# Hybrid attention in double items of both token tiles

## The reference

```python
def one_block(q_blk):                         # differential attention, 128 queries
    s = jnp.einsum('bqhcd,bkhcd->bhcqk', q_blk, k).astype(jnp.float32) * scale
    p = jax.nn.softmax(s, axis=-1)
    a = p[:, :, 0] - lam * p[:, :, 1]
    return jnp.einsum('bhqk,bkhe->bqhe', a.astype(v.dtype), v)
...
of = of * lax.rsqrt(jnp.mean(jnp.square(of), axis=-1, keepdims=True) + RMS_EPS)
...
m = jnp.maximum(jnp.max(s, axis=-1, keepdims=True), sk)      # windowed attention
e = jnp.exp(s - m)
p = e / (jnp.sum(e, axis=-1, keepdims=True) + jnp.exp(sk - m))
o = jnp.einsum('bnhgqk,bnkhd->bnqhgd', p.astype(v.dtype), vb)
```

## Time and profile before

| | |
|---|---|
| median of three runs | 1758.63 us (1757.71 to 1762.2) |
| profiled execution: span, and all that is known of its time | 1762.7 us |
| TensorE busy | 1706.5 us (97%) |
| VectorE, ScalarE, GpSimd busy | 921.5, 631.6, 107.9 us |
| attention of layer 0 | from about 250 to 294 us |
| attention of layer 1 | from about 744 to 790 us |

### The profile page before, as it was taken

How to read it: one execution, slowest core, us unless ns; L and a number is a source line. 1 busy time by engine, 2 the same in 40 slices (tenths; PEclk the granted TensorE clock), 3 DMA queues, 4 the chain that set the end, 5 groups by cost and what they waited for, 6 DMA issues and landing times.

```text
span 1762.7 us, 21725 instructions
## 1 busy us (share of the span) xinstructions
PE 1706.5 (97%) x8752; PEld 1235.5 (70%) x8752; DVE 921.5 (52%) x1313; ACT 631.6 (36%) x824; POOL 107.9 (6%) x89
## 2 busy tenths in 40 slices
PE   8999999999999999999999998999998999999996
PEld 7888877878878888878887787744443777644442
DVE  4754757675465546676685597511113667411113
ACT  4544444364434443443554364211112344211110
POOL 1000060000000000512000000000000000000000
PEclk9999999999999999989999999999999999999998
DMA  7555540645555545505554343999999443999995
GB/s 304 188 191 189 193 168 1 239 180 182 188 202 187 184 189 189 193 25 202 187 183 167 137 176 120 363 413 426 428 428 380 173 144 115 363 413 424 430 424 240
DMA packets 47667, 419.77 MB, mean 238 GB/s; under 512 B 5377, under 2 KB 5377, under 8 KB 9185
## 3 DMA queue, kind: packets, MB, share of 16 engines
q1 hardware_dynamic: 44064, 405.82, 59.0%
q0 software_dynamic: 3520, 12.78, 2.1%
HBM read 417.53 MB, written 1.05 MB: 237 GB/s over the span
## 4 chain that ended last, share of the span: by engine, by line
PE 81%; DVE 7%; DMA 6%; ACT 3%; POOL 1%; issue 1%; SPq 0%; DVEq 0%; POOLq 0%; ACTq 0%
PE hh L1282 10%; PE y L659 10%; PE y L660 10%; PE y L661 10%; PE hh L659 8%; PE hh L661 8%; PE hh L660 8%; DMA wide<-pairs 6%; PE turn L1192 2%; PE hh L1314 2%; PE turn L1314 2%; DVE w_lo L1921 2%; ACT w_hi L1469 1%; PE y L1326 1%; PE turn L779 1%; PE turn L691 1%
## 5 line engine op out<-in xcount | busy, mean ns | idle before, releaser
L1921 DVE TENSOR_TENSOR w_lo<-raw,w_hi 128x2048 fp32r<-128x2048 f32 x181 | 411.2, 2289 | 141.5 <-ACT w_hi L1469 140.8
L1469 ACT ACTIVATE w_hi<-raw 128x2048 fp32r<-128x2048 f32 x193 | 365.0, 1912 | 58.1 <-DMA raw<-units 58.0
L659 PE MATMUL hh<-w_hi,xt_hi 128*128 128x512 f32 x704 | 279.6, 397 | 4.4 <-ACT work L1721 2.1
L661 PE MATMUL hh<-w_hi,xt_lo 128*128 128x512 f32 x704 | 275.3, 391 | 0.0
L660 PE MATMUL hh<-w_lo,xt_hi 128*128 128x512 f32 x704 | 274.8, 390 | 0.0
L1282 PE MATMUL hh<-wide,work 128*64 128x512 f32 x880 | 196.0, 594 | 4.1 <-DMA wide<-pairs 4.1
L659 PE MATMUL y<-w_hi,xt_hi 128*128 128x512 f32 (+1 forms) x464 | 183.4, 395 | 4.8 <-DVE xt_lo L2470 3.1
L660 PE MATMUL y<-w_lo,xt_hi 128*128 128x512 f32 (+1 forms) x464 | 179.4, 387 | 0.0
L661 PE MATMUL y<-w_hi,xt_lo 128*128 128x512 f32 (+1 forms) x464 | 179.2, 386 | 0.0
L659 PEld LDWEIGHTS hh<-w_hi,xt_hi 128*128 128x128 f32 x704 | 132.7, 188 | 33.6 <-DVE xt_lo L2028 2.9
L661 PEld LDWEIGHTS hh<-w_hi,xt_lo 128*128 128x128 f32 x704 | 132.4, 188 | 28.3
(11 more groups left out here) (366 smaller groups left out, 1994.8 us busy)
## 6 DMA issues: line engine op xcount, KB each, us to landing
raw<-units SPq DMA_DIRECT2D x193, 1024.0 KB
wide<-pairs SPq DMA_DIRECT2D x81, 2048.0 KB
wide<-pairs SPq DMA_DIRECT2D x8, 1024.0 KB, 9.9
late<-pairs SPq DMA_DIRECT2D x7, 1024.0 KB
raw<-pairs SPq DMA_DIRECT2D x7, 1024.0 KB
spare<-pairs SPq DMA_DIRECT2D x2, 2048.0 KB
xt_wide<-pairs SPq DMA_DIRECT2D x2, 2048.0 KB
ln_gb<-ln_g POOLq DMA_DIRECT2D x6, 512.0 KB, 3.9
```

The source lines that it names most:

```text
L659: pe.matmul(dst, left[0], right[0], start=start, stop=False)
L661: return pe.matmul(dst, left[1], right[0], start=False, stop=stop)
L1469: act.activation(hi[r][:, :], raw[r][:, :], ACT.Copy).then_inc(hi_ready, 1)
L1921: dve.tensor_tensor(lo[r][:, :], raw[r][:, :], hi[r][:, :].bitcast(F32), ALU.subtract)\
```

## The change

TensorE, VectorE and ScalarE now work on double items j of both token tiles. `scores(j)` writes four score matrices, tile 0 into the first and tile 1 into the second half of each bank; `score[j % 2]` is reused by double item j + 2. `maxima(j)` is one reduction of 1024 columns into four maxima, and `combine(j)` computes the two ratios at once and then issues two weighted differences. The exponential buffers are four instead of two. The copies of the turned items are shared: the even ones (tile 0) go to ScalarE, the odd ones (tile 1) to VectorE, in the differential and in the windowed part. The squares for the norm move to GpSimd (`mix_squared`). The loop of TensorE goes `turn(i)`, `pv(i - 1)`, and after each odd i `scores(i // 2 + 2)`; `scores(0)` and `scores(1)`, now of four items, still stand in the middle of the last tile of the projection.

The diff, cut to its core (unchanged lines, new semaphores and the renumbered waits of `pv` are left out, and some indentation):

```diff
@@ -431,7 +432,7 @@
-e1 = carve(work, 11520, 2, 2, T)
+e1 = [carve(work, at, 2, T) for at in (11520, 12032, 13056, 13568)]
...
@@ -602,6 +603,9 @@
+        for t in range(TT):
+            pool.wait_ge(diff_read, TT * l + t + 1)
+            pool.tensor_tensor(rot[:, t], mix[:, t, 0:512], mix[:, t, 0:512], ALU.mult).then_inc(mix_squared, 1)
...
@@ -885,24 +889,27 @@
     def hybrid(l):
-        def scores(i):
-            t = i % 2
-            k_tile = i // 2 if i < 8 else 4 + (i - 8) // 4
-            if i >= 2:
-                pe.wait_ge(exp_ready, 16 * l + i - 1)
-            if i == 1:
+        def scores(j):
+            if j >= 2:
+                pe.wait_ge(exp_ready, 16 * l + 2 * j - 2)
+            if j == 1:
                 pe.wait_ge(tile_taken, seen(tile_taken, TT))
-            if i == 8:
+            if j == 4:
                 pe.wait_ge(col_ready, seen(col_ready, 2))
-            for c in range(2):
-                rows = slice(HD * c, HD * c + HD)
-                mm = pe.matmul(score[t][:, c, 0:T], qt1[rows, i // 2, t * P:(t + 1) * P], kt1[rows, k_tile, :],
-                               start=True, stop=i < 8)
-            if i >= 8:
-                other = slice((1 - t) * P, (2 - t) * P)
+            k_tile = j if j < 4 else 4 + (j - 4) // 2
+            for t in range(TT):
+                for c in range(2):
+                    rows = slice(HD * c, HD * c + HD)
+                    mm = pe.matmul(score[j % 2][:, c, t * T:(t + 1) * T], qt1[rows, j, t * P:(t + 1) * P],
+                                   kt1[rows, k_tile, :], start=t == 0, stop=t == 1 and j < 4)
+            if j >= 4:
                 pe.wait_ge(masks_ready, 6)
-                for c in range(2):
-                    mm = pe.matmul(score[t][:, c, other], ident_r[:, :], swa_far[:, t, other], start=False, stop=True)
+                for t in range(TT):
+                    other = slice((1 - t) * P, (2 - t) * P)
+                    for c in range(2):
+                        mm = pe.matmul(score[j % 2][:, c, t * T + (1 - t) * P:t * T + (2 - t) * P], ident_r[:, :],
+                                       swa_far[:, t, other], start=False, stop=t == 1)
             mm.then_inc(scores_ready, 1)
...
@@ -923,10 +930,7 @@
-            if i < 8:
-                pe.wait_ge(pt_ready, seen(pt_ready))
-            else:
-                pe.wait_ge(swa_pt, 8 * l + i - 7)
+            pe.wait_ge((pt_ready, odd_pt)[t], 8 * l + i // 2 + 1)
...
@@ -1595,30 +1599,35 @@
         def exps(i):
-            b = i % 2
-            act.wait_ge(neg_ready, seen(neg_ready))
-            if 2 <= i < 10:
-                act.wait_ge(prob_ready, 8 * l + i - 1)
-            elif i >= 10:
-                act.wait_ge(prob_turned, 16 * l + i - 1)
+            t, j = i % 2, i // 2
+            if t == 0:
+                act.wait_ge(neg_ready, seen(neg_ready))
+            if 4 <= i < 12:
+                act.wait_ge(prob_ready, 8 * l + i - 3)
+            elif i >= 12:
+                act.wait_ge(prob_turned, 16 * l + i - 3)
             for c in range(2):
-                head = i // 2 if i < 8 else 2 * ((i - 8) // 2) + c
-                neg, total = (neg_diff[:, b, c], diff_sum[:, b, c]) if i < 8 else (neg_swa[:, b], swa_sum[:, b])
-                ins = act.activation(e1[:, b, c], score[b][:, c, 0:T], ACT.Exp, bias=neg[:, head:head + 1],
-                                     accum_out=total[:, head:head + 1])
+                head = j if i < 8 else 2 * (j - 4) + c
+                neg, total = (neg_diff[:, t, c], diff_sum[:, t, c]) if i < 8 else (neg_swa[:, t], swa_sum[:, t])
+                ins = act.activation(e1[i % 4][:, c], score[j % 2][:, c, t * T:(t + 1) * T], ACT.Exp,
+                                     bias=neg[:, head:head + 1], accum_out=total[:, head:head + 1])
             ins.then_inc(exp_ready, 1)
...
             act.wait_ge(prob_turned, 16 * l + i + 1)
-            act.activation(pt1[:, i % 2, 0:T], turn_bank[i % 2][:, 0:T], ACT.Copy).then_inc(pt_ready, 1)
-        for i in range(16):
-            exps(i)
-            if i == 15:
-                act.wait_ge(sink_ready, l + 1)
-                act.activation(sink_e, sink_e, ACT.Exp).then_inc(sink_exp, 1)
-            if 2 <= i < 10:
-                copies(i - 2)
+            n_ = T if i < 8 else 2 * T
+            act.activation(pt1[:, 0, 0:n_], turn_bank[0][:, 0:n_], ACT.Copy).then_inc(pt_ready, 1)
+        for j in range(8):
+            exps(2 * j)
+            if j >= 2:
+                copies(2 * j - 2)
+            exps(2 * j + 1)
+            if j == 1:
+                copies(0)
+        copies(14)
+        act.wait_ge(sink_ready, l + 1)
+        act.activation(sink_e, sink_e, ACT.Exp).then_inc(sink_exp, 1)
         for b in range(2):
...
@@ -2117,28 +2126,31 @@
-        def maxima(i):
-            b = i % 2
+        def maxima(j):
             dve.wait_ge(scores_ready, seen(scores_ready))
-            s = score[b][:, :, 0:T]
-            if i < 8:
-                dve.tensor_reduce(neg_diff[:, b, :, i // 2], s, AX_X, ALU.max, negate=True).then_inc(neg_ready, 1)
+            s = score[j % 2][:, :, :].rearrange("p c (t k) -> p t c k", t=TT)
+            if j < 4:
+                dve.tensor_reduce(neg_diff[:, :, :, j], s, AX_X, ALU.max, negate=True).then_inc(neg_ready, 1)
             else:
-                two = slice(2 * ((i - 8) // 2), 2 * ((i - 8) // 2) + 2)
-                link(dve.tensor_reduce(nmax[:, b], s, AX_X, ALU.max, negate=True))
-                dve.tensor_tensor(neg_swa[:, b, two], nmax[:, b], neg_sink[:, l, two], ALU.min)                            .then_inc(neg_ready, 1)
-        def combine(i):
-            b, h = i % 2, slice(i // 2, i // 2 + 1)
-            dve.wait_ge(exp_ready, 16 * l + i + 1)
-            link(dve.reciprocal(ratio[:, b], diff_sum[:, b, 1, h]))
-            link(dve.tensor_scalar(ratio[:, b], ratio[:, b], diff_sum[:, b, 0, h], minus_lam[:, l:l + 1],
-                                   ALU.mult, ALU.mult))
-            if i >= 2:
-                dve.wait_ge(prob_turned, 16 * l + i - 1)
-            dve.scalar_tensor_tensor(out=p1[:, b], in0=e1[:, b, 1], scalar=ratio[:, b], in1=e1[:, b, 0],
-                                     op0=ALU.mult, op1=ALU.add).then_inc(prob_ready, 1)
+                two = slice(2 * (j - 4), 2 * (j - 4) + 2)
+                sinks = neg_sink[:, l, two].rearrange("p (o h) -> p o h", o=1).broadcast_to([P, TT, 2])
+                link(dve.tensor_reduce(nmax, s, AX_X, ALU.max, negate=True))
+                dve.tensor_tensor(neg_swa[:, :, two], nmax, sinks, ALU.min).then_inc(neg_ready, 1)
+        def combine(j):
+            dve.wait_ge(exp_ready, 16 * l + 2 * j + 2)
+            if j > 0:
+                dve.wait_ge(prob_ready, 8 * l + 2 * j)
+            link(dve.reciprocal(ratio, diff_sum[:, :, 1, j]))
+            link(dve.scalar_tensor_tensor(out=ratio, in0=ratio, scalar=minus_lam[:, l:l + 1], in1=diff_sum[:, :, 0, j],
+                                          op0=ALU.mult, op1=ALU.mult))
+            for t in range(TT):
+                i = 2 * j + t
+                if i >= 2:
+                    dve.wait_ge(prob_turned, 16 * l + i - 1)
+                dve.scalar_tensor_tensor(out=p1[:, t], in0=e1[i % 4][:, 1], scalar=ratio[:, t:t + 1], in1=e1[i % 4][:, 0],
+                                         op0=ALU.mult, op1=ALU.add).then_inc(prob_ready, 1)
...
@@ -2153,10 +2165,9 @@
-        def square(t):
-            dve.wait_ge(diff_read, TT * l + t + 1)
-            link(dve.tensor_tensor(rot[:, t], mix[:, t, 0:512], mix[:, t, 0:512], ALU.mult))
+        def sum_squares(t):
+            dve.wait_ge(mix_squared, TT * l + t + 1)
             dve.tensor_reduce(ssq[:, t], heads(rot[:, t]), AX_X, ALU.add).then_inc(squares, 1)
...
@@ -2170,26 +2181,24 @@
             dve.wait_ge(prob_turned, 16 * l + i + 1)
-            dve.tensor_copy(pt1[:, i % 2, :], turn_bank[i % 2][:, :]).then_inc(swa_pt, 1)
-        for i in range(16):
-            if i == 2:
+            n_ = T if i < 8 else 2 * T
+            dve.tensor_copy(pt1[:, 1, 0:n_], turn_bank[1][:, 0:n_]).then_inc(odd_pt, 1)
+        for j in range(8):
+            maxima(j)
+            if j >= 2:
+                copies(2 * j - 3)
+            if 1 <= j < 5:
+                combine(j - 1)
+            if j == 1:
                 values()
-            maxima(i)
-            if i >= 10:
-                copies(i - 2)
-            if 1 <= i < 9:
-                combine(i - 1)
-            if i in (9, 10):
-                read_diff(i - 9)
-            if i in (11, 12):
-                square(i - 11)
-            if i in (13, 14):
-                sub_norm(i - 13)
-        dve.wait_ge(neg_ready, seen(neg_ready, 16))
+            for t in range(TT):
+                if j >= 5:
+                    (read_diff, sum_squares, sub_norm)[j - 5](t)
+        dve.wait_ge(neg_ready, seen(neg_ready, 8))
```

(19 more changed lines are left out.)

## The result

| kernel | median us | runs | ratio to before (95% interval) | mean clock of the profiled run |
|---|---|---|---|---|
| before | 1761.98 | 5 | 1 | 0.988 |
| changed | 1803.48 | 5 (1794.98 to 1805.66) | 1.0236 (1.0219 to 1.0254) | 0.973 |

The change makes the kernel 41.5 us slower. Slower was forecast, but by 24.4 us; 1803.5 lies just above the range's upper end of 1801. The forecast of 1783 stood on 1758.6 for the kernel before, the median of three runs; with two more runs that median is 1762.0, so 3.4 us of the miss are the base and 17.1 the change. The profiled run took 1803.48 us with a span of 1801.4.

The account below looks back on a forecast made before the run. It took a dependency ring over two items, not any engine's work, to bound the differential part. Base 1758.6 plus 20.4 for the new order and 4 for low clock gave 1783 us; range 1776 to 1793, 8 in 10 1768 to 1801.

Parts of the forecast that it names:

- The ring through combine, turn, product, scores and maxima: Differential part: each double's combination must return as scores before the next, 5.6 us per double against 3.47.
- The windowed part, 6.0 per double at full clock: Windowed attention: odd product waits for VectorE's copy behind the maxima; 6.0 us per double, 1.4 more.
- The start: Start of attention: GpSimd's low part holds combine(0)'s second difference until 260.27, values end at 262.3, double 2's scores at 265.0.
- The squares on GpSimd: Norm squares on GpSimd: 1.15 us each, two end at 288 before the sums at 290.7, so they cost nothing.
- The sum, 20.4: Both layers' attention without further low-clock stretches: last product of layer 0 at 302.4 instead of 292.20, 10.2 us per layer.
- The clock, 4 us: TensorE in both attention stages: two low-clock stretches per layer beyond the start's, about 1 us each.
- the clock stays low: Rival, chance 0.15: new gaps keep TensorE at 1.2 GHz for most of both stages, 13 us per layer, 1805 us.
- The profiled span: Whole kernel before: span 1762.7 us, three-run median 4.1 below, about what layer 1's slow end costs.

Follow-up runs that it names:

- e8_fill_both: Changed kernel plus 12 unread matmuls at each of five TensorE waits per layer, in the differential and windowed parts: 1783.79 us, 1.0143 of before.
- e5_low_parts_moved: `e1_scores_ahead` with the low parts of units 7 and 8 per attention layer on VectorE instead of GpSimd: 1744.15 us, 0.9903 of before.
- e1_scores_ahead: Changed kernel with scores(j + 2) issued ahead of turn(2j) instead of behind turn(2j + 1) on TensorE: 1748.15 us, 0.9922 of before.
- e6_squares_back: `e1_scores_ahead` with the two squares of the norm back on VectorE instead of GpSimd: 1756.04 us, 0.9977 of before.
- e2_fill: Changed kernel plus 12 unread matmuls ahead of turn(2), turn(4) and turn(6) per layer, where TensorE waits: 1790.19 us, 1.0164 of before.
- e7_copies_unshared: `e1_scores_ahead` with copies as before the change, ScalarE all differential and VectorE all windowed items: 1766.97 us, 1.0022 of before.

## Why the prediction was right in kind and wrong in size

- *The ring through combine, turn, product, scores and maxima.* Right. The waits stand where it said, the order undone removes them, and its 5.6 us, 6.3 for the double with masks, were measured as 5.4, 5.8 and 6.0 once the clock was kept. (Its terms add up to 5.7.)
- *The windowed part, 6.0 per double at full clock.* Right: in `e8_fill_both` the odd products of items 9 and 11 start 6.17 us apart (290.62 and 296.79).
- *The start.* Right: one difference slips in, the other ends at 260.95, the values at 262.3, the scores of double 2 at 265.1. The row had given nearly all of it; a bit of luck is in the last figure, since the product took 0.74 and the scores 2.08 where 1.0 and 1.65 were assumed. `e5_low_parts_moved` shows that GpSimd's instruction is the holder. By the Trainium skill ("SBUF — State Buffer", Who interferes with whom) a VectorE instruction with two SBUF inputs and a GpSimd instruction that reads SBUF exclude each other for the whole instruction; the runs agree, down to an operation of two columns (1.46 against 0.22 us).
- *The squares on GpSimd.* 2.04 us for two, forecast 2.3; hidden, as forecast. What the prediction did not see is that they are worth something, about 4 us, once TensorE's order is right.
- *The sum, 20.4.* Right: 19 us between the runs at the higher clocks, and in layer 0 the last product at 302.24 against 302.4, with the steps before it within 0.4.
- *The clock, 4 us.* This is the step that failed. "I take two such stretches per layer beyond the start's, about 1 us each: 4 in all." The runs showed about 24: the last product of the changed kernel starts 12.5 us behind that of `e8_fill_both` in layer 0 and 24.0 behind it in layer 1, near the bound of 13 per layer that the prediction named for the whole stage. The argument for the small number was that the clock stayed at 1.00 in 280 to 290 with TensorE busy 8.45 of 10. But TensorE's waits there were under 1 us, and the new ones are 2.5 us in each ring of 5.6; the nearer rows were those of 259 to 264, where the clock fell after a single wait of 1.65 us. Those rows do not make a fall certain either: `e1_scores_ahead` waits 1.22 and 0.88 us at that place and its clock stays at 1.00. The rival "the clock stays low" had 0.15 and gives 1805, within 2 us of the measured time; part of that closeness is luck, since it stood on the base of 1758.6.
- *The profiled span.* The prediction took the 4.1 us between it and the median for layer 1's slow end. That this is the cause is not shown, since the faster runs have no trace; over 23 runs the kernel before spreads from 1755.71 to 1764.08, at clocks of 0.994 to 0.989. A forecast to a few us must say which of these it stands on.

The clock's cause is shown as far as this: filling the waits with unread matmuls brings it back and shortens the kernel. Every fall in the attention stages of these traces follows a wait of TensorE, but not every wait is followed by a fall: 1.32 and 1.31 us in the two layers of `e6_squares_back` end differently, and equal programs differ from run to run. What decides it stays open.

## What to carry to other kernels

When items are joined into larger ones, ask where the next item's first step stands in each queue: put it ahead of the steps that wait for this item, or the joined pipeline has nothing in flight. Price a new wait of TensorE twice: by its length, and by what the matmuls of the stage cost at 1.2 GHz; if the clock already falls behind shorter waits in the trace, take the stage at low clock as a likely case, not as the bound. And a run with unread matmuls in the gaps tells in one go how much of a loss is the order and how much the clock.

## What the runs showed of the hardware

- Twelve matmuls of 256 columns that nothing reads, three times per layer, made the kernel 13.3 us faster (`e2_fill` against the changed kernel).
- The same program varied by 13 to 14 us between runs on one chip, in step with its mean clock (`e8_fill_both`, `e7_copies_unshared`), while the two kernels whose attention kept the clock at 1.00 in the profiled run varied by 2 to 4 us (`e1_scores_ahead`, `e5_low_parts_moved`).
- Equal waits of TensorE need not have equal effects: after 1.32 us the clock stayed at 1.00, after 1.31 us in the other layer of the same run a product took 1.81 us instead of 1.00 (`e6_squares_back`).
- GpSimd holds back a VectorE operation with two SBUF inputs even if it has two columns: 1.46 us against 0.22 (`e5_low_parts_moved`).
